# A decoder layer on one core: the router stage as one written-out tile pipeline, gathers with a bound, final loads at once

## The reference

```
y = concat([ya, yb, yc]) @ w_out                       # 1024 x 1024
x = x + g1 * rmsnorm(y, norm_post_mix)
h = rmsnorm(x, norm_pre_ffn) * (1 + sc2) + sh2
scores = sigmoid(h @ w_router)                         # 64 experts in 8 groups
biased = scores + e_bias
# 4 best groups by the sum of their 2 best, then the 8 best experts in them
top_w = top_s / (sum(top_s) + 1e-20) * 2.5
routed[t] = sum over its 8 experts of top_w * (silu(h @ w1[e]) * (h @ w3[e])) @ w2[e]
shared = (silu(h @ ws1) * (h @ ws3)) @ ws2             # hidden width 256, as each expert
x = x + g2 * rmsnorm(routed + shared, norm_post_ffn)
```

## Time and profile before

| | us |
|---|---|
| median of 3 runs (lowest, highest) | 2318.48 (2313.07, 2322.95) |
| the profiled execution: its time | 2318.01 |
| its span | 2316.3 |
| PE busy | 1915.6 (83%) |
| DVE busy | 1328.5 (57%) |
| ACT busy | 1008.2 (44%) |
| POOL busy | 466.9 (20%) |
| DMA | 416.40 MB, mean 180 GB/s |

### The profile page before, as it was taken

One profiled execution on the slowest core, in us unless ns is written; L12 is line 12 of the kernel. 1 busy time (PEld: TensorE's weight loads), 2 busy tenths in 40 slices (PEclk: granted clock), 3 DMA queues, 4 the chain that ended last, 5 costly groups with the idle time before them and its releaser, 6 DMA issues. The chain is left out here.

```text
span 2316.3 us, 31665 instructions
## 1 busy us (share of the span) xinstructions
PE 1915.6 (83%) x8701; PEld 1372.7 (59%) x8702; DVE 1328.5 (57%) x2415; ACT 1008.2 (44%) x1810; POOL 466.9 (20%) x336
## 2 busy tenths in 40 slices
PE   2799997773887957998619999999999999999990
PEld 2688875552777853444316666666666676666660
DVE  6476615874677732333415666666766766666673
ACT  3222214652443412222215556655655665556562
POOL 0000000003222100212421333322323332233230
PEclk9899999985989968999859999999999999999995
DMA  8056202003110026342236998989989999899956
GB/s 338 1 181 227 81 6 70 16 16 146 39 40 6 6 93 243 70 71 62 56 112 199 301 301 249 300 243 345 341 233 288 346 359 288 242 305 303 321 112 236
DMA packets 130205, 416.40 MB, mean 180 GB/s; under 512 B 18276, under 2 KB 30909, under 8 KB 127054
## 3 DMA queue, kind: packets, MB, share of 16 engines
q1 hardware_dynamic: 96270, 288.76, 35.4%
q0 software_dynamic: 32720, 122.64, 20.4%
q10 hardware_dynamic: 1152, 4.19, 0.4%
HBM read 337.85 MB, written 77.94 MB: 180 GB/s over the span
## 5 line engine op out<-in xcount | busy, mean ns | idle before, releaser
L2006 DVE TENSOR_TENSOR w_low<-w_experts,w_high 128x1024 fp32r<-128x1024 f32 x392 | 453.9, 1220 | 131.0 <-ACT w_high L1968 120.2
L1968 ACT CAST w_high<-w_experts 128x1024 fp32r x392 | 381.8, 1046 | 102.0 <-issue 100.9
L2082 PE MATMUL ps_y<-w_experts,actT 128*128 x768 | 355.1, 606 | 37.9 <-issue 27.4
L2059 PE MATMUL ps_h<-w_high,xT_high 128*128 128x512 f32 x776 | 315.7, 407 | 4.4 <-DVE xT_low L2012 4.4
L2059 PE MATMUL ps_h<-w_high,xT_low 128*128 128x512 f32 x776 | 307.4, 396 | 0.0
L2059 PE MATMUL ps_h<-w_low,xT_high 128*128 128x512 f32 x776 | 307.3, 396 | 0.0
L1949 POOL DMA_INDIRECT acc<-y_rows,scatter_idx x96 | 152.4, 1588 | 703.0 <-DVE idx L1999 350.2
L2082 PEld LDWEIGHTS ps_y<-w_experts,actT 128*128 128x128 f32 x768 | 140.8, 193 | 185.2 <-issue 185.1
L1990 ACT COPY y_rows<-ps_y 128x512 f32<-128x512 f32 x96 | 56.4, 587 | 284.5 <-PE ps_y L2082 284.5
L1932 POOL DMA_INDIRECT gathered<-h,idx x99 | 167.4, 1691 | 44.3 <-issue 29.6
L2059 PEld LDWEIGHTS ps_h<-w_high,xT_high 128*128 128x128 f32 x776 | 147.3, 190 | 36.8 <-issue 2.9
(11 more groups left out here) (414 smaller groups left out, 3221.0 us busy)
## 6 DMA issues: line engine op xcount, KB each, us to landing
w_experts<-in_exp_w SPq DMA_DIRECT2D x384, 512.0 KB
qT<-in_w_ada POOLq DMA_DIRECT2D x16, 1024.0 KB, 5.3
w_raw<-in_w_in SPq DMA_DIRECT2D x24, 512.0 KB, 7.8
w_ada<-in_w_ada SPq DMA_DIRECT2D x8, 1024.0 KB, 12.0
pb<-pb_tile SPq DMA_DIRECT2D x16, 256.0 KB, 2.4
pb_cur<-pb SPq DMA_DIRECT2D x8, 512.0 KB, 3.9
pb_prev<-pb SPq DMA_DIRECT2D x8, 512.0 KB, 5.2
w_out<-in_w_out SPq DMA_DIRECT2D x1, 4096.0 KB, 16.1
```

Of the source, the lines that this page charges most:

```text
L1968: act.copy(w13_s[par][0][:, which, k], w13[:, bass.ds(w, 1), which, k].squeeze(1)).then_inc(w_high, 1)
L2006: dve.tensor_tensor(w13_s[par][1][:, which, k], w13[:, bass.ds(w, 1), which, k].squeeze(1), w13_s[par][0][:, which, k], ALU.subtract).then ...
L2059: q = pe.matmul(ps_h[:].rearrange("p (a n) -> p a n", a=2), xT[a][:, k, :], w13_s[par][z][:, :, k, :], start=(k == 0 and m == 0), stop=(k ...
L2082: q = pe.matmul(ps_y[n][:], aT[:, k, :], w2[:, bass.ds(w, 1), k, n * BANK:(n + 1) * BANK].squeeze(1), start=(k == 0), stop=(k == FC - 1))
```

## The change

There are five edits.

1. `norm_route` is written out in ten rounds (r from -1 to 9) rather than in a loop, and each step has a semaphore of its own. In round r, PE projects tile r+1, transposes the mixed output of tile r+2, does the up projection of tile r-2, transposes h of tile r, places tile r-1, routes tile r, and ends the shared expert of tile r-2. The other engines have an order of the same kind.
2. ACT's wait for the zeroed rows stands before the copy of the first shared output, no longer before its first copy. Down products go to p0 and p1 rather than t0 and t1, and the router's to t1.
3. `schedule` is no block of its own: its constants are loaded at the start of `norm_route`, and its steps stand in the last round.
4. The gathers of `experts` get `bounds_check=S - 1, oob_is_err=False`: entries above 1023 are left out.
5. `finish` loads all eight acc tiles at once; the gains and x2 are loaded at the end of `experts`, x2 into weight slots 1 and 2, once their up weights have been read for the last time; SP issues the stores.

```diff
-        PE = Stages(sem("r_pe_done"), ["h2T.0", "route.0", "up.0", "h2T.1", "route.1", "aT.0", "up.1", "down.0", "aT.1", "down.1", "pos.0", "pos.1"])
...
+            for t in range(2, 4):
+                sp.wait_ge(yT_mm, t - 1)
+                load_y(t)
...
         def _(act):
             load_exp_and_ln(nc, act)
-            act.wait_ge(zero_out, 48)
...
+            def shared_out(t):
+                w = lane[t % 2]
+                if t == 0:
+                    act.wait_ge(zero_out, 48)
...
+                for n, src in enumerate((w.p0, w.p1)):
+                    act.wait_ge(down_mm, 2 * t + n + 1)
+                    act.copy(w.ysh[:, n * BANK:(n + 1) * BANK], src[:]).then_inc(ysh_done, 1)
...
+            y_copy(0)
+            y_copy(1)
+            for r in range(-1, NT + 2):
+                if r + 1 < NT:
+                    y_norm(r + 1)
+                if 0 <= r and r + 2 < NT:
+                    y_copy(r + 2)
+                if r + 1 < NT:
+                    x_norm(r + 1)
+                if 0 <= r < NT:
+                    h_copy(r)
+                if r >= 2:
+                    shared_sig(r - 2)
+                if 0 <= r < NT:
+                    score_exp(r)
+                if r >= 2:
+                    shared_out(r - 2)
...
@@ DVE
+            for r in range(-1, NT + 2):
+                if r + 1 < NT:
+                    x_rows(r + 1)
+                    h_scaled(r + 1)
+                if r == NT + 1:
+                    block_counts()
+                if r >= 2:
+                    shared_arg(r - 2)
+                if r + 1 < NT:
+                    h_rows(r + 1)
+                if r == NT + 1:
+                    block_ends()
+                if 1 <= r <= NT:
+                    places(r - 1)
+                if r >= 2:
+                    shared_act(r - 2)
+                if 0 <= r < NT:
+                    logits(r)
+                if r >= 2:
+                    copy_act(r - 2)
+                if 0 <= r < NT:
+                    select(r)
+            block_rows()
...
@@ PE
+            def transpose_h(t):
+                w = lane[t % 2]
+                pe.wait_ge(h2_done, t + 1)
+                if t + 2 < NT:
+                    pe.wait_ge(yT_done, t + 3)
...
+            def down(t):
+                w = lane[t % 2]
+                pe.wait_ge(aT_done, t + 1)
...
@@ experts, SP and POOL
+            sp.dma_start(keep["post2"][:], dr["rows"][:, 5 * D:6 * D].partition_broadcast(P)).then_inc(keep["post_in"], 16)
+            for half in range(2):
+                sp.wait_ge(w_low, sp.value_load(tab[0:1, 3, E - SLOTS + 1 + half:E - SLOTS + 2 + half], min_val=4, max_val=4 * BLOCKS))
+                for t in range(4 * half, 4 * half + 4):
+                    sp.dma_start(keep["x2"][half][:, t % 4, :], dr["x2"][t * P:(t + 1) * P, :]).then_inc(keep["x2_in"][half], 16)
...
-                pool.indirect_dma_start(xg[j][:], None, dr["h2"], bass.IndirectOffsetOnAxis(ap=idx[j][:], axis=0)).then_inc(xg_in[j], 16)
+                pool.indirect_dma_start(xg[j][:], None, dr["h2"], bass.IndirectOffsetOnAxis(ap=idx[j][:], axis=0),
+                                         bounds_check=S - 1, oob_is_err=False).then_inc(xg_in[j], 16)
...
@@ finish, SP
+            for t in range(NT):
+                sp.dma_start(a[t][:], dr["acc"][t * P:(t + 1) * P, :]).then_inc(acc_in[t], 16)
+            for t in range(NT):
+                sp.wait_ge(sums, t + 1)
+                sp.dma_start(out[0][t * P:(t + 1) * P, :], x2[t]).then_inc(outs, 16)
```

More of the change, by code:

```diff
@@ L1559, in _, with y_copy @@
-            for j in range(2):
-                project_copy(0, j)
-            with act.Fori(0, TURNS - 1) as i:
-                turn(i, False)
-                step.restart()
-            turn(TURNS - 1, True)
+            eps = keep["eps"][:, 0:1]
+            def y_copy(t):
+                w = lane[t % 2]
+                act.wait_ge(yT_mm, t + 1)
+                if t >= 2:
+                    act.wait_ge(proj_mm, t - 1)
+                act.copy(w.yT[:, 0:4, :], k4(w.t0[:]))
+                act.copy(w.yT[:, 4:8, :], k4(w.t1[:])).then_inc(yT_done, 1)
@@ L1665, in turn @@
-                PE.wait(dve, i, "pos.1")
-                both(lambda w: tt(w.left[:], w.t0[:, 0:E], list_at[:], ALU.add))
-                both(lambda w: tt(w.left[:], w.left[:], w.sel[:], ALU.mult))
-                both(lambda w: dve.max(w.top[:], w.left[:]))
-                for j in range(2):
-                    w = lane[j]
-                    step.then(tt(seen[:], seen[:], w.sel[:], ALU.add))
-                    V.done(ts(w.dest[:], w.top[:], -1.0, None, ALU.add), f"pos.{j}")
-                V.wait(dve, i, "pos.1")
@@ L1832, in _ @@
+            block_rows()
             dve.wait_ge(rows_T, 1)
-            step.then(dve.tensor_copy(lists[:, 0:P], ps_c[:]))
+            step.then(dve.tensor_copy(lists[:, 0:P], ps_c[:, 0:P]))
         @block.tensor
@@ new lines, in project @@
+            def project(t):
+                w = lane[t % 2]
+                pe.wait_ge(yT_done, t + 1)
+                if 2 <= t < 4:
+                    pe.wait_ge(xn_done, t - 1)
+                for n in range(2):
+                    if t >= 4:
+                        pe.wait_ge(ysh_done, 2 * (t - 4) + n + 1)
+                    for k in range(KC):
+                        q = mm((w.p0, w.p1)[n][:], w.yT[:, k, :], w_out[:, k, n * BANK:(n + 1) * BANK], start=(k == 0), stop=(k == KC - 1))
+                q.then_inc(proj_mm, 1)
@@ new lines, in place, with route @@
+            def place(t):
+                w = lane[t % 2]
+                pe.wait_ge(sel_done, t + 1)
+                pe.wait_ge(h2T_done, t + 1)
+                if t:
+                    pe.wait_ge(pos_done, t)
+                mm(w.t0[:, 0:E], ones[:], seen[:], start=True, stop=False)
+                mm(w.t0[:, 0:E], strict[:], w.sel[:], start=False, stop=True).then_inc(pos_mm, 1)
+            def route(t):
+                w = lane[t % 2]
+                pe.wait_ge(h2T_done, t + 1)
+                for k in range(KC):
+                    q = mm(w.t1[:, 0:E], w.h2T[:, k, :], w_r[:, k, :], start=(k == 0), stop=(k == KC - 1))
+                q.then_inc(route_mm, 1)
@@ new lines, in transpose_act @@
+            def transpose_act(t):
+                w = lane[t % 2]
+                pe.wait_ge(act_done, t + 1)
+                for k in range(FC):
+                    q = pe.transpose(w.p0[:, F + k * P:F + (k + 1) * P], w.acts[:, k * P:(k + 1) * P], ident[:])
+                q.then_inc(aT_mm, 1)
+            def down(t):
+                w = lane[t % 2]
+                pe.wait_ge(aT_done, t + 1)
+                for n in range(2):
+                    for k in range(FC):
+                        q = mm((w.p0, w.p1)[n][:], w.aT[:, k, :], ws2[:, k, n * BANK:(n + 1) * BANK], start=(k == 0), stop=(k == FC - 1))
+                    q.then_inc(down_mm, 1)
@@ L1849, in _ @@
             pe.wait_ge(rows_in, 16)
-            pe.transpose(ps_c[:], rows[:], ident[:]).then_inc(rows_T, 1)
+            pe.transpose(ps_c[:, 0:P], list_rows[:], ident[:]).then_inc(rows_T, 1)
 def experts(nc, io, dr, keep):
@@ L2246, in build @@
         with nc.sbuf_tensor("w_slots", [P, SLOTS, 3 * KC * F], F32):
-            schedule(nc, io, dr, keep)
+            keep["x2"] = [nc.alloc_sbuf_tensor_at(f"x2_kept{half}", [P, 4, D], F32, offset=slots_at + (1 + half) * 3 * KC * F * 4) for half in range(2)]
             experts(nc, io, dr, keep)
-        finish(nc, io, dr, keep, out)
+            finish(nc, io, dr, keep, out)
 DUMP = ["rows", "pb", "ymix", "x2", "h2", "acc", "out_x"]
```

655 lines of the change are left out of this document (286 added, 369 removed).

## The result

The changed kernel takes 2226.35 us (median of 4 runs, 2221.93 to 2237.15), the kernel before 2315.88 on the same chip; the ratio is 0.9612, with a 95% interval of 0.9585 to 0.9640. The forecast was 2228. The profiled execution takes 2225.57 us, its span is 2223.8, 92.5 less than before. The total came out right, the terms did not all: the stretch from the first projection to the first expert index gave 10.8 us less than forecast, the experts 13.3 more. (Stages are cut at TensorE's first projection, the first expert index and the first acc load of the last stage.)

A forecast was written before the change was run, and what follows sets the result against it. In the expert stage PE is busy 479 of 500 us and the DMA engines 0.94 of the time. Terms -66.4 (route and schedule), -12 (gathers), -12.4 (finish), +1 (early loads) sum to -89.8: 2318.0 to 2228 us, range 2206 to 2258.

The forecast's parts named there:

- Part 1: Start of route stage: first projection no longer waits behind ACT's wait for the zero DMAs; -21.6 us.
- Part 2: Route stage's new rounds: full rounds of 31.5 us, gains there going to filling and draining; +1.2 us, 268.0 for 266.8.
- PE waits anew in each round: Rival, 13%: in-order DVE and ACT delay the shared expert's chain, 3 us more in 8 rounds, +24; 2252 us.
- Part 3: Block schedule folded into the route stage, lists and counts under PE's last rounds; 46.0 us saved before the first expert index.
- two readings: Gap from 1170.91 to 1183.33 before the schedule: landing of lists, or partly the loops' exit with an instruction fetch.
- The reserve of "3 us": Before the experts: if the gap is list landing, the list-row gather starts 3 us later than its rows are computed.
- Part 4: Expert stage: gathers leave out unfilled rows, 35% of their bytes, shortening stalls in 21 blocks; -12 us.
- relief of the DMA engines: Rival, 13%: less traffic also lands weights and scatters earlier, half the expert stalls go; -30 rather than -12, 2210 us.
- The bound of 57: Expert stage: most that cutting gathers could gain, if every stall goes (61 us less the cold first block).
- The loss side, a dearer issue: Expert gathers: bound test lengthens POOL's descriptor work, up to +93 us; rival at 4%, 2333 us.
- late gathers stay late: Rival, 20%: the engine with most rows sets landing, so blocks half full or more gain nothing; gather term -3, 2237 us.
- Part 5: Final stage: only acc loaded there, gains and x2 loaded under the experts; 30.2 us, -12.4.

The follow-up runs named there:

- the fillers: Changed kernel with 54 unused 256-column products put into TensorE's idle time in the route stage: 2213.48 us, ratio 0.9529.
- the two later runs with fillers: Changed kernel with fillers and the limit also on scatters, 2196.49 us; the same with the last two rounds turned, 2191.32 us.
- the last rounds turned: Against the kernel with fillers and cut scatters: last tile's up projection before the previous tile's transposes, ten fillers removed; 2191.32 us, ratio 0.9449.

## Why the prediction was right, and where it was wrong

**Part 1** held: PE's first projection starts 3.5 us after its transposes, -21.8 for -21.6, and the wait put back costs 27.

**Part 2, the rounds, was mis-sized.** PE needed 280.1 us from the first projection to the end of its last down projection (859.63 to 1139.74), not 268.0: 3.1 more up to the end of round 1, 6.2 in rounds 2 to 6, 2.8 in the last three. The waits of the full rounds were no larger than forecast (0.77, 0.22, 0.52). Full rounds took 30.4 to 35.5 us for 31.5; the one of 35.5 passes the prediction's own sign of being wrong, 34. What failed is that each matmul was priced at its duration in the old loop, as if durations did not depend on the waits around them. With the fillers the same path takes 260.6 us, and a full round 30.4, less than the 31.5 of the sum. So the term of part 2, +1.2, was +13.3 as measured, and is -6.2 with the fillers. The rival *PE waits anew in each round* had half its size (+12 of +24) but not its mechanism.

The old loop had given a hint. In the very turn that the prediction priced, one of the two up projections takes 8.78 us, not 7.03; its window shows the clock below 1.00, so 1.75 of the "6 us of waits" in that turn were clock:
```profile
1047.85 8.78 PE L1717 MATMUL rbank<-shared_w,h2T 128*128 128x512 f32 x16
```
```profile
1048.00:1056.00 8.00, 8.00 (x16) 3.34 (x15) 5.20 (x6) 1.65 (x4) 6.24 (x6) 0.79 0.59 80
```
There were four such falls of 3.4 us in the old loop, in which PE waited 1.1 to 1.5 us at a time. In the new rounds there are nine, of 3.4 to 10.2 us, with shorter waits in the full rounds. So the length of a wait by itself does not tell whether the clock falls.

**Part 3** was right in its result and half right in its reasons. The index comes 5.1 us after PE's end (6.4 in the sum). The gap after GpSimd's last issue, which the prediction left between two readings, is half the lists' landing and half GpSimd's drain; the drain was in neither reading. Both lie under PE's work in the new order, until something shortens PE's path. The Trainium skill (Runtime: NRT & Kernel Launch, Instruction fetch mechanics) was cited for a fetch at the loops' exit; writing the loop out changed nothing, and of the 12.4 us only 0.6 are neither landing nor drain, so no row here shows such a fetch. The reserve of "3 us" given for the landing did not come into play: the lists had landed at 1129.6, and the list rows were computed later (1134.99).

**Part 4 was mis-sized the other way:** -24.3 with the early loads, for -11, and 17 to 27 us by all runs. The step that failed is the price of a stalled block: 0.65 us of transfer saved in each of 21 blocks. The table by filled places shows that a partly filled gather loses most of its stall (34.4 us of stalls became 9.5). Landings that come 0.1 to 0.9 us earlier brought stalls of 1.1 to 4.4 us down to between 0 and 2.2. The prediction had the reason in hand, that a late gather costs more than it is late since the table loads behind it come late as well, and did not use it in the sum. Both kinds of relief were there that the forecast held apart, at the gathers and (by the waits for weights, 9.8 to 3.2 us) beside them, so the rival *relief of the DMA engines* (-30) was nearer than the forecast. The bound of 57 was not reached, because the 37 gathers with 110 places or more keep their 27 to 30 us. The loss side, a dearer issue, did not show.

The rival *late gathers stay late* named the descriptor swizzle of the Trainium skill (DMA: Bandwidth & Descriptors) as its ground. Its outcome was wrong, but the packet records do not speak against that mapping, if the row packets are given to the gathers by counting them in order of time. The two gathers with 4 filled rows move them one after another, never two at once. Gathers with 64 filled rows or fewer have at most 10 row packets in flight, full ones up to 19. That is what one sees if neighbouring places share an engine, and the lower 64 places half of the engines. What failed is the step from there to "gains nothing".

**Part 5** held: -13.6 for -12.4, tiles of 2.46 us for 2.7; the +1 for early loads did not show.

**The sum** was right to 2 us by luck: +12 in part 2 stood against -13 in part 4. The total alone would have confirmed both.

## What to carry to other kernels

When a new order is priced with durations of the old one, read the granted clock beside each duration: short waits that are free by themselves can halve the clock of the work behind them, and useless products in the waits gave most of it back here. A transfer that lands late should be priced by the wait it ends, not by its bytes: leaving out rows nobody needs removed most of the stalls, and the scatter ahead in the same queue was worth another 12 to 16 us. Where a gap has no row, look for what the view leaves out, such as the drain at the end of a block. Check a right total by stages, and undo each part alone; two errors of a dozen us had cancelled here.

## What the runs showed of the hardware

- TensorE was at 0.50 of its clock for 3.4 to 6.8 us at a time in full rounds, where its waits were 0.2 to 0.8 us, and for 10.2 us in rounds 0 and 1, where they were 2.3 to 3.3 us. With fillers of 0.43 us each it stayed at 1.00 up to 1126.7: 18 us of 285. In each of the two later runs with fillers it still fell once, for 3.4 us.
- In the packet records of the experts' stage a row added into DRAM by the scatter (4096 bytes) takes 362 ns of a DMA engine, a gathered row (4352 bytes) 177 ns. With the limit the gathers have 8192 such packets instead of 12672, and 4480 more packets of 4 bytes, 11 ns each.
- From the end of the issue of the last eight list transfers (128 single words each) to the end of GpSimd's wait for them it took 5.9 us in the kernel before, 7.1 with GpSimd's loop written out, 3.7 in the changed kernel and 6.3 with the last rounds turned. In the last of these runs the queue's packets all start before 1110, and the wait ends at 1114.4.
- GpSimd's drain at the end of a block took 5.7 to 7.0 us in every block in which it had issued DMAs, but for the old schedule with its single fetch (3.0), and at most 0.7 us in the others. Behind the experts it stands open in both kernels: in the changed one the other engines are through at 2185.6, the drain runs from 2189.5 for 5.78 us, and the last stage starts at 2195.5.
